# Two transformer blocks on one core: the low parts of fourteen gate weights are made by GpSimd in place of VectorE

## The reference, cut to what matters

```python
h = rmsnorm(x, norm_mix)
u = h @ w_in                                       # 7552 columns
gates = sigmoid(u[..., RWKV_COLS + DA_COLS:])      # 2 x 1024 columns
y_a = rwkv7_branch(u[..., :RWKV_COLS], ...)        # 8 heads, a delta rule forward and backward
y_b = diff_attn_branch(u[..., RWKV_COLS:RWKV_COLS + DA_COLS], ...)
x = x + (gates[0] * y_a + gates[1] * y_b) @ w_out
```

## Time and profile before

| | |
|---|---|
| median of three runs | 1664.79 us (1664.04 to 1665.77) |
| span of the profiled execution, first to last instruction | 1662.5 us |
| its own time, beside the span | not given apart; the median of the runs is 2.3 us above the span |
| PE busy | 1633.7 us, 98% |
| DVE busy | 1059.4 us, 64% |
| ACT busy | 732.1 us, 44% |
| POOL busy | 98.8 us, 6% |
| granted TensorE clock, mean | 0.998 of full speed |
| the delta rule's block | from about 213 to 464 us of the span |

### The profile page before, as it was taken

How to read it: one execution, slowest core, us unless ns; L and a number is a source line. 1 busy time by engine, 2 the same in 40 slices (tenths; PEclk the granted TensorE clock), 3 DMA queues, 4 the chain that set the end, 5 groups by cost and what they waited for, 6 DMA issues and landing times. The chain is left out here.

```text
span 1662.5 us, 30282 instructions
## 1 busy us (share of the span) xinstructions
PE 1633.7 (98%) x12906; PEld 1292.8 (78%) x12906; DVE 1059.4 (64%) x1508; ACT 732.1 (44%) x1105; POOL 98.8 (6%) x123
## 2 busy tenths in 40 slices
PE   9999999999999999999999999999999999999997
PEld 6666777777767888888888788886578888888887
DVE  6867589888657577577765773365986654343434
ACT  5444555534265443231324553337775543232323
POOL 0000000000000100001111000031101000000001
PEclk9999999999999999999999999999999999999999
DMA  6212231112145343446563222320002233233321
GB/s 229 85 51 75 83 117 42 41 42 98 36 171 183 127 164 136 156 162 218 192 216 112 86 92 77 114 89 26 20 2 89 86 105 101 90 101 101 101 90 51
DMA packets 51318, 172.81 MB, mean 104 GB/s; under 512 B 6129, under 2 KB 9329, under 8 KB 50417
## 3 DMA queue, kind: packets, MB, share of 16 engines
q1 hardware_dynamic: 41456, 134.71, 24.1%
q0 software_dynamic: 9728, 36.18, 6.5%
HBM read 160.64 MB, written 8.39 MB: 102 GB/s over the span
## 5 line engine op out<-in xcount | busy, mean ns | idle before, releaser
L376 PE MATMUL pair<-h_hi,w_hi 128*128 128x512 f32 x1008 | 402.2, 399 | 1.5 <-DVE w_lo L422 1.0
L378 PE MATMUL pair<-h_hi,w_lo 128*128 128x512 f32 x1008 | 393.0, 390 | 0.0
L377 PE MATMUL pair<-h_lo,w_hi 128*128 128x512 f32 x1008 | 392.9, 390 | 0.0
L422 DVE TENSOR_TENSOR w_lo<-w_raw,w_hi 128x1024 fp32r<-128x1024 f32 (+1 forms) x224 | 265.2, 1188 | 147.7 <-ACT w_hi L401 147.5
L401 ACT CAST w_hi<-w_raw 128x1024 fp32r<-128x1024 f32 (+1 forms) x224 | 220.9, 992 | 229.0 <-PE pair L378 212.1
L376 PEld LDWEIGHTS pair<-h_hi,w_hi 128*128 128x128 f32 x1008 | 189.3, 188 | 55.6 <-issue 16.4
L377 PEld LDWEIGHTS pair<-h_lo,w_hi 128*128 128x128 f32 x1008 | 189.5, 188 | 39.9 <-issue 2.8
L378 PEld LDWEIGHTS pair<-h_hi,w_lo 128*128 128x128 f32 x1008 | 189.3, 188 | 40.2
L376 PE MATMUL pair<-ff_f_hi,w_hi 128*128 128x512 f32 (+1 forms) x536 | 204.3, 381 | 0.6 <-DVE w_lo L422 0.6
L378 PE MATMUL pair<-ff_f_hi,w_lo 128*128 128x512 f32 (+1 forms) x536 | 203.6, 380 | 0.0
L377 PE MATMUL pair<-ff_f_lo,w_hi 128*128 128x512 f32 (+1 forms) x536 | 203.6, 380 | 0.0
(11 more groups left out here) (465 smaller groups left out, 2465.6 us busy)
## 6 DMA issues: line engine op xcount, KB each, us to landing
w_raw<-in_w_ff SPq DMA_DIRECT2D x128, 512.0 KB, 3.3
mod_w<-in_w_mod POOLq DMA_DIRECT2D x48, 512.0 KB, 3.7
w_raw<-in_w_in SPq DMA_DIRECT2D x22, 512.0 KB, 3.4
w_raw<-in_w_gate SPq DMA_DIRECT2D x16, 512.0 KB, 3.3
w_raw<-in_w_out SPq DMA_DIRECT2D x16, 512.0 KB, 3.3
w_raw<-in_w_rwkv SPq DMA_DIRECT2D x15, 512.0 KB, 3.3
w_raw<-in_w_da SPq DMA_DIRECT2D x12, 512.0 KB, 4.6
w_raw<-in_w_ple_gate SPq DMA_DIRECT2D x8, 512.0 KB, 3.3
```

The source lines that it names most:

```text
L376: nc.tensor.matmul(out, w_hi, x_hi, start=(k == 0), stop=False)
L377: nc.tensor.matmul(out, w_hi, x_lo, start=False, stop=False)
L378: last = nc.tensor.matmul(out, w_lo, x_hi, start=False, stop=(k == kt - 1))
L422: nc.vector.tensor_tensor(lo[:, s % SPLIT_SLOTS, 0:cols], pr.raw[:, w % RAW_SLOTS, 0:cols], hi[:, s % SPLIT_SLOTS, 0:cols].bitcast(F32), A ...
```

## The change: what it does

The low parts of gates 2 to 15 leave VectorE's list and go to GpSimd's: behind the issue of the store of gate j's result GpSimd waits for the high part of gate j + 2 and makes its low part, the same subtraction on the same operands. TensorE waits on the same semaphore as before. `low_point` goes. The loop on GpSimd now runs over 16 gates, with a store for the first 15 and a low part for the first 14.

```diff
-    def low_point(self, j):
-        at, pair = self.point_of[j] + 3, self.point_of[j] + 3 - self.start_of_pairs
-        if pair >= 0 and pair % self.PAIR == 2:
-            return at + (2 if pair // self.PAIR == RT - 1 else 4)
-        return at
-
...
                 pr.nc.vector.tensor_tensor(self.staged, self.bank(j), self.rstd, ALU.mult).then_inc(self.out, 1)
-            if self.low_point(j) == point and j + 2 < self.JOBS:
-                self.low(dve, j + 2)
 
     def pool(self, pool):
-        for j in range(self.JOBS - 1):
-            pool.wait_ge(self.out, j + 1)
-            pool.dma_start(self.spill[:, j, :], self.staged).then_inc(self.stored, 16)
+        for j in range(self.JOBS):
+            if j < self.JOBS - 1:
+                pool.wait_ge(self.out, j + 1)
+                pool.dma_start(self.spill[:, j, :], self.staged).then_inc(self.stored, 16)
+            if j + 2 < self.JOBS:
+                self.low_pool(pool, j + 2)
+
+    def low_pool(self, pool, j):
+        pool.wait_ge(self.hi_made, j + 1)
+        self.pr.nc.gpsimd.tensor_tensor(self.weight_low(j), self.weight(j), self.w_hi[:, j % 2, :].bitcast(F32), ALU.subtract).then_inc(self.lo_made, 1)
```

## The result

The changed kernel took 1670.15 us (median of 6 runs, 1668.71 to 1671.0) against 1664.79 for the kernel before beside it: ratio 1.0033, 95% interval 1.0022 to 1.0044, so some 5.4 us slower. The profiled execution took 1670.38, its span 1668.2: 5.7 us more than before's span. The rwkv part of the changed file stands one line higher, the gates' own lines six: L1671 of before is L1670 here, L1464 is L1463, L1783 is L1782, L1817 is L1816, L1271 is L1270, the high part L1072 is L1066, the store L1098 is L1091; GpSimd's low part is L1097.

A forecast was written before the change was run, and what follows sets the result against it. TensorE, 98% busy, was taken as the bound, with at most 3.5 us to regain from VectorE. Preparation 1.5 + pairs 2.9 - relief 0.5 = +3.9 on span 1662.5 gave 1666.4, plus 2.3 to the median: 1668.7; range 1663.5 to 1674.

The forecast's parts named there:

- GpSimd's 2.4 us: Each low part on GpSimd: a 128x1024 subtraction taking 2.4 us, between 2.07 and 2.70; fourteen make 34 us.
- Rival 4: GpSimd's subtraction to fp32r is slower, 3.5 us each, making the loss +8.5 and the time 1673.3; chance 0.08.
- The hold is what decides: GpSimd's low part waits for VectorE's running two-SBUF-operand product, then holds the next for its own length; this cost decides.
- Three pairs, 1.1 + 0.9 + 0.9 = 2.9: Gates 6, 9, 12: L1670 held, VectorE 2.2 us late, TensorE stalls before L1464; 2.9 us in all.
- Preparation, 1.5: Gates 2 to 4: holds in keys and `scaled` delay products TensorE waits for; 1.5 us.
- the first case: Gate 4: GpSimd comes behind the last L1671, first factors 1.2 us late; in the second it comes ahead, together 3.3.
- Gates 5, 8, 11, 14, 15 and 7, 10, 13 for nothing: The first five meet no hold; the other three hold one key sum 0.5 to 0.9 us, costing TensorE nothing.
- Relief 0.5: Outside the preparation, TensorE's waits that VectorE ends shrink by 0.5 us, bounds 0 and 1.8.
- rival 2: VectorE paces this stretch, so 17 us off it give TensorE back 3.5 us: 1661.3; chance 0.06.
- Unchanged from there to the end: After the delayed places, the time to the end of the program stays the same.
- Rival 1: TensorE hides it: holds are shorter or low parts fall beside PSUM instructions; +0.3 to 1, 1665.4; chance 0.22.
- Rival 3: GpSimd's first arithmetic, at gate 2, is late behind its configuration: one more 2.2 us hold, +6.1, 1670.9; chance 0.12.

The follow-up runs named there:

- no low parts: Low parts of gates 2 to 15 left out on both engines, so the result is wrong; against the kernel before: 1663.37 us, ratio 0.9994.
- a write alone: Changed kernel with GpSimd filling the low tile with zeros in place of the subtraction; 1663.45 us, ratio 0.9993 to the kernel before.
- the wait in the run: Changed kernel with VectorE waiting before its third product of `scaled` for its own two before; 1672.4 us, ratio 1.0049 to the kernel before.
- the repeat: The changed kernel measured again, unedited; 1669.24 us, ratio 1.003 to the kernel before.
- gates 2 to 4 on VectorE: Changed kernel with the low parts of gates 2, 3 and 4 given back to VectorE; 1666.57 us, ratio 1.0014 to the kernel before.
- behind the starts: Changed kernel, gates 2 to 4 back on VectorE; GpSimd's low parts 6, 9, 12 also wait for VectorE's pair starts; 1663.87 us, ratio 0.9997 to before.
- pairs on VectorE: Changed kernel with the low parts of gates 6, 9 and 12 given back to VectorE; 1665.85 us, ratio 1.0013 to the kernel before.
- pieces: Changed kernel with each GpSimd low part in four instructions of 256 columns; 1664.58 us, ratio 1.0006 to the kernel before.
- the last kernel above: Changed kernel with gates 2 to 4 back on VectorE and GpSimd's other eleven low parts in four pieces each; 1663.57 us, ratio 0.9995 to before.

## Why the prediction was right, point by point

- **GpSimd's 2.4 us**: 2.36 to 2.40 where nothing is in its way. Rival 4 had no ground. The estimate from the figure of the Trainium skill (page "GPSIMD Engine Reference", section "3.1 Elementwise"), 2.25, was the worse one. "Up to 3 at gates 3, 6, 9, 12" is wrong for the last three: 3.94.
- **The hold is what decides**: right. Without GpSimd's subtractions the loss is gone (no low parts, a write alone), and a product or a copy is held for nearly the low part's length.
- **Three pairs, 1.1 + 0.9 + 0.9 = 2.9**: measured 1.2, 1.1 and 1.15 in the shifts (2.8 by the medians). The place was right, the instruction was not, and the rule that a low part waits only for the running product failed here: I had GpSimd in behind L1669 of before, holding a product; it waited for the run's end and held the copies. That the price came out alike is luck in part: the copies happen to stand in the same list ahead of L1817, so the delay is 2.1 us in place of 2.2. The wait put in the run gave the picture that I had drawn, at 1.35 each.
- **Preparation, 1.5**: the profile has 1.60, from gate 3's hold as forecast (L1667 at 227.10), and for gate 4 the first case: the copies at 234.81 and no product. But I had priced that case at 1.2, and came to 1.5 by a share of the second, which did not occur; the agreement to 0.1 us is luck. In time it is worth more, 2.1 us by the medians. The step that was missing is TensorE's clock (below): it is in some executions and not in others, and no row of before has an idle time so long.
- **Gates 5, 8, 11, 14, 15 and 7, 10, 13 for nothing**: right, all eight together -0.5 us; a key sum is held 0.7 us at each of gates 7, 10 and 13, within the 0.5 to 0.9 forecast.
- **Relief 0.5**: mis-sized. It shows as 0.48 and 0.5 at 328.58 and 386.64, so 1.0 in all, where "no low parts" has 1.75 at 384 and 0.97 at the end. Of rival 2's 3.5 us the medians of all kernels here show at most 0.9.
- **"Unchanged from there to the end"**: not so in this profile, but not shown to be the change's. The shift grows by 1.6 us behind the third pair: 0.54 by L1284, 0.2 at L1432, and the rest at L376, where TensorE is idle for 0.65 us. In the repeat it falls by 0.5 behind the third pair. L376 waits behind a low part of the projection's weights, whose transfers run at a DMA share of 1.04 to 1.06; its idle time is 0.31 in the repeat, 1.07 with the wait in the run, and 0.44 with no low parts at all, so GpSimd's reads do not make it. Why it differs is open.
- **Rival 1**: false. Gate 6's request and the products beside it are both some 1.7 us later than before (L1668 at 277.96, L1669 of the earlier trace rows at 276.29), so the one still falls into the other. **Rival 3**: false. The configuration lies right behind the first store at 215.4, and gate 2's low part starts 0.09 us behind its high part. With gates 2 to 4 on VectorE the configuration stands at 246.2, and the first low part starts 1.4 us behind it (the timeline of "behind the starts") at its normal 2.37. The 6 us for a first call that the Trainium skill has (page "GPSIMD Engine Reference", section "2.1 Instruction dispatch") do not show here; the measurement decides.

The sum of the profile: 1.60 + 1.2 - 0.48 + 1.13 - 0.5 + 1.15 = 4.1 at the third L1463, and 0.54 + 1.06 behind it = 5.7. The forecast's +3.9 was the first of these. The repeat comes to its 4.9 in another way: 2.80 + 1.10 - 0.25 + 1.15 - 0.52 + 1.14 = 5.4 at the third L1463, and -0.5 behind it. The term that the forecast lacked and a trace explains is the clock, 1.2 us where it falls.

## What to carry to other kernels

Work on GpSimd is not free just because GpSimd is idle. What reads SBUF holds VectorE's products of two SBUF operands, and even a write alone held a copy and a TENSOR_SCALAR: ask which VectorE instructions stand beside it, and what TensorE has queued when they end 2.2 us late. If it must lie beside a run of products, put it behind the product that releases the next engine (here one wait on a semaphore that existed), or cut it into pieces. And ask what is gained at all: here VectorE gave up 17 us of work, and the most that any version made of it was 0.9 us by the medians, no more than the scatter of the runs.

## What the hardware showed that I had not expected

- **GpSimd stays out of an unbroken run.** In three pairs it waited 1.56 us through two products that it could have come between, and got in when the run ended; with one short pause it got in there. In the preparation it came between two products without a pause (2.87 us for L1667), few instructions behind VectorE's last pause. What sets this is open. The Trainium skill, page "SBUF — State Buffer", section "Who interferes with whom", has issue order decide; GpSimd's low part stands from 278.15, ahead of L1669 at 278.57 and L1670 at 279.17, and both went first. The measurement decides.
- **Small and one-input instructions are held too.** A copy of 64x8, 0.17 us by itself, took 2.23 four times (once in the preparation, once in each of three pairs), and a TENSOR_SCALAR of 128x512 2.56, where it takes 0.52:

```profile
L1675 DVE COPY rw_ends<-rw_pin x8: 167/1200/2233, 234.8 to 398.3; 64x8 f32<-64x8 f32 x8
...
220.18 2.56 DVE L1648 TENSOR_SCALAR x<-x,params,derived 128x512 f32<-128x512 f32 x1
```
  The prediction had only instructions of two SBUF operands in mind.
- **Some 3 us of idle TensorE can cost its clock.** Behind 2.93 us of idle (the repeat), 2.93 (pairs on VectorE) and 3.05 (the wait in the run) the clock was at 0.50 for 3.4, 6.8 and 3.4 us (in the second it fell 0.7 us before TensorE went on); behind 3.11 (the changed kernel) and 2.27 (pieces) it stayed at 1.00 in the profiles. It costs about 1.2 us (2.80 less 1.60). Of "pairs on VectorE" the five runs with a mean clock of 0.998 have the median 1665.56, the six at 0.996 and 0.997 about 1667.1. Of "pieces" three have 0.997 and 1666.1 to 1667.2, the other eight 0.998 and at most 1665.0. The spread of such a kernel grows with it: 1664.64 to 1668.3, against 1662.88 to 1664.57 for the last kernel above, with no such idle time. What sets whether the clock falls is open.
